# A two-layer decoder trunk: eight conditioning items to VectorE, routing by token tile, first expert outside the loop

## The reference, cut to what matters

```python
def modulate(x, shift, scale):
    return x * (1 + scale[:, None, :]) + shift[:, None, :]

c_act = jax.nn.silu(c)
h = x
for layer in range(2):
    mod = c_act @ w_ada[layer] + b_ada[layer]            # 1024 x 6144, one row
    sh_m, sc_m, gt_m, sh_f, sc_f, gt_f = jnp.split(mod, 6, axis=-1)
    u = modulate(rms_norm(h, g_mix[layer]), sh_m, sc_m)
    y = even_mixer(u, ...) if layer == 0 else dsa_mixer(u, ...)
    h = h + gt_m * y
    u = modulate(rms_norm(h, g_ffn[layer]), sh_f, sc_f)
    y = swiglu(u, ...) if layer == 0 else moe_swiglu(u, ...)
    h = h + gt_f * y
return rms_norm(h, g_final)

def moe_swiglu(u, w_router, b_router, w_gate, w_up, w_down):
    logits = tok @ w_router + b_router                   # 8 experts
    top_val, top_idx = lax.top_k(logits, 2)
    gates = jax.nn.softmax(top_val, axis=-1)
    combine = einsum('tk,tke->te', gates, one_hot(top_idx, 8))
    for e in range(8):
        out = out + combine[:, e:e+1] * swiglu(tok, w_gate[e], w_up[e], w_down[e])
```

## Time and profile before

| | us |
|---|---|
| median of 3 runs | 1614.06 |
| lowest, highest | 1613.65, 1614.63 |
| the profiled execution | 1612.1 |
| its span, first to last instruction | 1610.3 |

### The profile page before, as it was taken

How to read it: one execution, slowest core, us unless ns; L and a number is a source line. 1 busy time by engine, 2 the same in 40 slices (tenths; PEclk the granted TensorE clock), 3 DMA queues, 4 the chain that set the end, 5 groups by cost and what they waited for, 6 DMA issues and landing times.

```text
span 1610.3 us, 21805 instructions
## 1 busy us (share of the span) xinstructions
PE 1517.3 (94%) x7379; PEld 1173.7 (73%) x7380; DVE 1254.9 (78%) x1715; ACT 1047.7 (65%) x1381; POOL 71.9 (4%) x99
## 2 busy tenths in 40 slices
PE   4999989999799878999999999999999999999997
PEld 2645458888585457887887888888888888888885
DVE  6896335544583238989989989989989989989987
ACT  3105444443457527788788788788788788788785
POOL 5251000000000000000000000000000000000000
PEclk9999999999899979999999999999999999999999
DMA  9734975544467657999999999999999999999970
GB/s 305 262 105 177 345 266 204 209 147 171 154 210 248 223 203 263 367 372 351 363 373 349 369 367 349 366 372 360 355 371 366 350 369 364 349 381 365 351 300 28
DMA packets 205176, 474.92 MB, mean 295 GB/s; under 512 B 5252, under 2 KB 11702, under 8 KB 204998
## 3 DMA queue, kind: packets, MB, share of 16 engines
q1 hardware_dynamic: 202656, 466.80, 79.5%
q0 software_dynamic: 1824, 6.33, 1.2%
q10 hardware_dynamic: 646, 1.16, 0.3%
HBM read 472.17 MB, written 2.10 MB: 295 GB/s over the span
## 4 chain that ended last, share of the span: by engine, by line
PE 81%; ACT 5%; DVE 4%; issue 2%; ACTq 0%; DVEq 0%
PE ps L821 23%; PE ps L823 23%; PE ps L822 22%; PE ps L827 3%; DVE w_lo L1972 2%; PE ps L1340 2%; PE ps L1094 2%; ACT work L1868 1%; PE ps L846 1%; ACT uT L1624 1%; ACT w_hi L1611 1%; ACT uT L1633 1%; PE ps L1462 0%; PE ps L866 0%; PE ps L1463 0%
## 5 line engine op out<-in xcount | busy, mean ns | idle before, releaser
L1972 DVE TENSOR_TENSOR w_lo<-ring,w_hi 128x1024 fp32r<-128x1024 f32 (+2 forms) x572 | 665.9, 1200 | 122.9 <-ACT w_hi L1611 104.7
L1611 ACT ACTIVATE w_hi<-ring 128x1024 fp32r<-128x1024 f32 (+2 forms) x572 | 593.0, 1047 | 215.0 <-PE ps L823 211.4
L821 PE MATMUL ps<-w_hi,e_hi 128*128 128x512 f32 x896 | 357.5, 399 | 9.7 <-DVE w_lo L1972 9.7
L823 PE MATMUL ps<-w_hi,e_lo 128*128 128x512 f32 x896 | 350.6, 391 | 0.0
L822 PE MATMUL ps<-w_lo,e_hi 128*128 128x512 f32 x896 | 349.9, 390 | 0.0
L1972 DVE TENSOR_TENSOR w_lo<-ring_more,w_hi 128x1024 fp32r<-128x1024 f32 x192 | 230.5, 1222 | 12.5 <-ACT w_hi L1611 9.7
L1611 ACT ACTIVATE w_hi<-ring_more 128x1024 fp32r<-128x1024 f32 x192 | 202.8, 1061 | 48.6 <-PE ps L823 48.6
L821 PEld LDWEIGHTS ps<-w_hi,e_hi 128*128 128x128 f32 x896 | 168.9, 188 | 46.0 <-DVE w_lo L1972 13.2
L823 PEld LDWEIGHTS ps<-w_hi,e_lo 128*128 128x128 f32 x896 | 168.7, 188 | 36.6
L822 PEld LDWEIGHTS ps<-w_lo,e_hi 128*128 128x128 f32 x896 | 169.2, 189 | 33.2
L821 PE MATMUL ps<-w_hi,eT_hi 128*128 128x512 f32 x448 | 176.7, 394 | 5.6 <-DVE w_lo L1972 5.6
(11 more groups left out here) (286 smaller groups left out, 1566.6 us busy)
## 6 DMA issues: line engine op xcount, KB each, us to landing
ring<-in_moe_w_gate SPq DMA_DIRECT2D x48, 2048.0 KB, 9.7
ring<-in_moe_w_up SPq DMA_DIRECT2D x40, 2048.0 KB, 9.8
ring<-in_moe_w_down SPq DMA_DIRECT2D x32, 2048.0 KB, 8.9
ring<-in_w_ada SPq DMA_DIRECT2D x24, 2048.0 KB, 9.2
ring_more<-in_moe_w_down SPq DMA_DIRECT2D x24, 2048.0 KB, 10.3
ring_more<-in_moe_w_up SPq DMA_DIRECT2D x16, 2048.0 KB, 9.8
ring_more<-in_moe_w_gate SPq DMA_DIRECT2D x8, 2048.0 KB, 7.8
ring<-in_ff_w_gate SPq DMA_DIRECT2D x5, 2048.0 KB, 7.9
```

What stands on the lines that cost most here:

```text
L821: mm(o, xh, wh, start=start, stop=False)
L823: return mm(o, xl, wh, start=False, stop=stop)
L1611: fn(w, src, ACT.Copy).then_inc(hi_ready, 1)
L1972: V.tensor_tensor(w_lo[0:n, c, 0:f], src, w_hi[0:n, c, 0:f].bitcast(F32), ALU.subtract).then_inc(lo_ready, 1)
```

## The change

It has three parts.

1. **Conditioning.** Items 12 to 19 are multiplied by DVE inside the first four feed-forward blocks, two items a block, eight instructions an item (`gemv`); PE adds over partitions and adds the bias at the end of the feed-forward (`gemv_gate` for items 16 and 17 in place of `matvec` 14 and 15, `gemv_columns` for the other six). Items 14 to 19 are loaded between the feed-forward's weights. Items 20 to 23 are left for the attention, in every second head pair. Items 12 to 23 now come in the order shift, scale, gate of the mixer, then shift, scale, gate of the feed-forward. DVE's and SP's loops over blocks are written out. The slots of `e_out`, set free by `matvec` 12 before, are now set free by the first product of `rows_of`.
2. **Routing by token tile.** The logits of tile 0 are computed before tile 1 is transposed, DVE finds its experts at once, and the position products are split. The one-hot matrix of expert 0 comes right after the positions, the combination weights follow it, and the tables of overfull experts (`job_tables`) come after expert 0.
3. **First expert.** ACT and DVE do expert 0 outside their loops. ACT makes the high parts of gate 0 before the softmax of routing, DVE the low parts between the tokens' halves; PE waits for the tokens' halves one by one.

Four items fewer lie in the static stream, so `n_item[0] % 5` is 1 at L539 and `moe_order` becomes slots 1, 2, 3, 4, 0.

```diff
-        parts1 = ada[:, 0:4 * 512].rearrange("p (i n) -> p i n", i=4)
+        parts1 = ada[:, 0:8 * 512].rearrange("p (i n) -> p i n", i=8)
...
-        for (sec, half), back in zip(HALVES[2:4], (3, 1)):
+        for (sec, half), back in zip(HALVES1[2:8], (3, 1) * 3):
             n_item[0] = n_then - back
-            ada_item(1, sec, half)
+            ada_item(1, sec, half, "gemv")
...
-        for sec, half in ((2, 0), (2, 1), (3, 0), (3, 1), (4, 0), (4, 1), (5, 0), (5, 1)):
+        for sec, half in HALVES1[8:]:
             ada_item(1, sec, half)
```

SP, the loads of the feed-forward:

```diff
+            mid_at = {(2 + i // 2, ("down", "up")[i % 2]): e for i, e in enumerate(static_mid)}
+            for b in range(2, FB):
                 for k in FFK:
+                    sp.wait_ge(lo_ready, (b - 2) * CB + (ff_chunks1 + ff_chunk[k] + NCI))
+                    ff_load(k, b, FW if b < FB - 1 else FL)
+                    if (b, k) in mid_at:
+                        load(mid_at[b, k])
...
-            sp.wait_ge(router_done, 1)
+            sp.wait_ge(router_done, 2)
```

PE, the conditioning:

```diff
+            def gemv_columns(i, bank, c):
+                row = ada_items[i][1]
+                mm(ps[bank][:, c:c + 4], bias_rows[0:BROWS, :], ident[0:BROWS, row:row + 4], start=True, stop=False)
+                for q in range(4):
+                    w = mm(ps[bank][:, c + q:c + q + 1], parts1[:, i - 12, q * P:(q + 1) * P], ones[:, 0:1],
+                           start=False, stop=q == 3)
+                return w
+            def gemv_gate(i, bank):
+                pe.wait_ge(gemv_done, i - 11)
+                row = ada_items[i][1]
+                mm(ps[bank][:, :], ones, parts1[:, i - 12, :], start=True, stop=False)
+                for q in range(4):
+                    w = mm(ps[bank][:, q * P:(q + 1) * P], ident[0:BROWS, row + q:row + q + 1].broadcast_to([BROWS, P]),
+                           bias_rows[0:BROWS, :], start=False, stop=q == 3)
+                w.then_inc(mod_summed, 1)
...
-            matvec(12, 2)
...
-            pe.wait_ge(part_ready, 13)
             rows(ff_first["up"][2], (2, 3), FW, range(NCI))
-            matvec(13, 6)
             ff_block(0, True)
...
-            matvec(14, 0)
-            matvec(15, 1)
+            gemv_gate(16, 0)
+            gemv_gate(17, 1)
...
-            pe.wait_ge(part_ready, 16)
+            pe.wait_ge(gemv_done, 8)
             for i in range(4):
-                w = columns_of(12 + i, parts1[:, i, :], 2, 4 * i)
-            w.then_inc(mod_summed, 1)
+                gemv_columns(12 + i, 2, 4 * i)
+            gemv_columns(18, 2, 16)
+            gemv_columns(19, 2, 20).then_inc(mod_summed, 1)
```

PE, the attention, where now only every second pair has a conditioning item:

```diff
-                matvec(16 + pair, 6)
+                if pair % 2 == 0:
+                    matvec(20 + pair // 2, 6)
...
-                ada_step(pair)
+                if pair % 2 == 0:
+                    ada_step(pair // 2)
```

PE, routing:

```diff
+            pe.wait_ge(late_in, 16 * 2)
+            router(0).then_inc(router_done, 1)
             norm(3, 1)
-            pe.wait_ge(late_in, 16 * 2)
-            router(0)
             router(1).then_inc(router_done, 1)
             pe.wait_ge(member_ready, 1)
             mm(ps[5][:, 0:E], tri, member(0), start=True, stop=True)
-            mm(ps[5][:, E:2 * E], tri, member(1), start=True, stop=False)
-            mm(ps[5][:, E:2 * E], ones, member(0), start=False, stop=True)
-            mm(ps[5][:, 2 * E:3 * E], ones, member(0), start=True, stop=False)
-            mm(ps[5][:, 2 * E:3 * E], ones, member(1), start=False, stop=True).then_inc(pos_done, 1)
+            mm(ps[5][:, E:2 * E], ones, member(0), start=True, stop=False)
+            pe.wait_ge(member_ready, 2)
+            mm(ps[5][:, E:2 * E], tri, member(1), start=False, stop=True).then_inc(pos_done, 1)
+            mm(ps[4][:, 2 * E:3 * E], ones, member(0), start=True, stop=False)
+            mm(ps[4][:, 2 * E:3 * E], ones, member(1), start=False, stop=True).then_inc(pos_done, 1)
```

PE, in the gather of expert 0, ahead of `slot_tokens`:

```diff
+                if first:
+                    pe.wait_ge(info_first, 1)
```

PE, in the expert:

```diff
+                        if kind == "gate" and b == 0 and c % 2 == 0:
+                            pe.wait_ge(e_ready, g * 2 + (c // 2 + 1))
-                pe.wait_ge(e_ready, g * 2 + 2)
```

ACT:

```diff
-                if t:
-                    part_out(12, parts1[:, 0, :], 2)
...
-            part_out(13, parts1[:, 1, :], 6)
...
-            part_out(14, parts1[:, 2, :], 0)
-            part_out(15, parts1[:, 3, :], 1)
+            gate_out(0, 0, 0, 10)
+            gate_out(0, 1, 1, 11)
...
+            item_high(moe_c0, 0, moe_fill0[0] + 16, moe_chunk)
             act.wait_ge(gap_ready, 1)
             fn(rt[:, :, 40:41], rt[:, :, 41:42], ACT.Exp).then_inc(gap_exp, 1)
             fn(stat[:, 30:31], eps[:, 0:1], ACT.Silu)
...
-            slots_in(0)
-            slots_high(0)
-            with act.Fori(0, E) as e:
+            for i in range(2):
+                slots_in(0, (i,))
+                slots_high(0, (i,))
+            expert(0, 0, True, True)
+            with act.Fori(1, E) as e:
```

DVE:

```diff
+            def gemv(i, k):
+                (ap, got), _ = ada_items[i]
+                acc = parts1[:, i - 12, :]
+                if k == 0:
+                    dve.wait_ge(fill[got[0]], got[1])
+                    w = V.tensor_scalar(acc, ap[:, 0, :], c_col[:, 0:1], None, ALU.mult)
+                else:
+                    dve.wait_ge(gemv_steps, (i - 12) * (KD - 1) + k)
+                    w = V.scalar_tensor_tensor(acc, ap[:, k, :], c_col[:, k:k + 1], acc, ALU.mult, ALU.add)
+                if k == KD - 1:
+                    w.then_inc(gemv_done, 1)
+                else:
+                    w.then_inc(gemv_steps, 1)
```

DVE, in `ff_block(i)`, with `a = 12 + 2 * i`:

```diff
+                split("gate", 0, (a, 0))
+                split("gate", 1, (a, 1))
                 mids(i * NT, q)
+                split("gate", 2, (a, 2))
+                split("gate", 3, (a, 3))
                 midT_low(i * NT)
+                for c in range(NCI):
+                    split("down", c, (a, 4 + c))
+                for c in range(NCI):
+                    split("up", c, (a + 1, 2 * c), (a + 1, 2 * c + 1))
...
+            gate_low(0, 1)
+            slots_low(0, (0,))
+            gate_low(2)
+            slots_low(0, (1,))
+            gate_low(3)
             step(V.memset(ps[4][:, :], 0.0))
             step(V.memset(ps[5][:, :], 0.0))
...
-            select(0, 0, 0)
-            slots_low(0)
-            with dve.Fori(0, E) as e:
+            expert(0, 1, 0, True, True)
+            job_tables()
+            with dve.Fori(1, E) as e:
```

More of the change, by code:

```diff
@@ L487, in trunk @@
         ff_first = ff_static(("gate", "up"), 0)
-        ada_item(1, *HALVES[0])
+        HALVES1 = [(sec, half) for sec in range(6) for half in range(2)]
+        ada_item(1, *HALVES1[0], "gemv")
         n_item[0] += 1
-        ada_item(1, *HALVES[1])
+        ada_item(1, *HALVES1[1], "gemv")
         static_before = list(stream)
@@ L1861, in _, with slots_in @@
             UF = FB * NT
-            def slots_in(g):
-                for i in range(2):
+            def slots_in(g, halves_=(0, 1)):
+                for i in halves_:
                     act.wait_ge(gather_done, g * 2 + (i + 1))
@@ L2342, in _ @@
                     mask_max(n + 3, selneg)
-                if pair == 6:
-                    columns(1, 1, 16, 7)
+                if pair == 3:
+                    dve.wait_ge(mod_summed, 14)
+                    V.scalar_tensor_tensor(mod_a[:, 1, :], ps[7][:, 0:KD], 1.0, g_col[:, 3, :], ALU.add,
+                                           ALU.mult).then_inc(mod_ready, 1)
             for t in range(NT):
@@ L2360, in _ @@
             for t in range(NT):
-                step(V.max_index(top_i[:, t, :], top[:, t, :], lg[:, t, :]))
-            step.wait()
-            step(V.tensor_copy(rt[:, :, 24:26], top_i[:, :, 0:2]))
-            V.tensor_tensor(rt[:, :, 41:42], top[:, :, 1:2], top[:, :, 0:1], ALU.subtract).then_inc(gap_ready, 1)
-            step.wait()
-            for t in range(NT):
+                dve.wait_ge(router_done, t + 1)
+                chained(V.tensor_tensor(lg[:, t, :], ps[4 + 2 * t][:, 0:E], b_r[:, :], ALU.add))
@@ new lines, in _ @@
+                V.tensor_tensor(rt[:, t, 16:24], rt[:, t, 0:8], rt[:, t, 8:16], ALU.add).then_inc(member_ready, 1)
+            V.tensor_tensor(rt[:, :, 41:42], top[:, :, 1:2], top[:, :, 0:1], ALU.subtract).then_inc(gap_ready, 1)
+            dve.wait_ge(member_ready, 2)
+            dve.wait_ge(pos_done, 1)
+            for t in range(NT):
+                step(V.scalar_tensor_tensor(possel[:, t, 0:E], ps[5][:, t * E:(t + 1) * E], 1.0, rt[:, t, 16:24], ALU.add, ALU.mult))
+            step.wait()
@@ new lines, in _ @@
+            chained(V.tensor_scalar(possel[:, :, 0:E], possel[:, :, 0:E], -1.0, None, ALU.add))
+            dve.wait_ge(pos_done, 2)
+            for t in range(NT):
+                w = V.tensor_scalar(sel[:, t, :], iota(P), possel[:, t, 0:1], None, ALU.is_equal)
+                if t == 0:
+                    step(w)
```

(17 more changed lines are left out.)

138 lines of the change are left out of this document (61 added, 77 removed).

## The result

The changed kernel takes 1598.39 us (median of four runs, 1597.3 to 1600.59) against 1614.35 (four runs) for the kernel before on the same chip: ratio 0.9898, 95% interval 0.9886 to 0.9911. I had forecast 1590.5 and a range of 1584.0 to 1597.5. The sign is right, the gain is not: 16 us where 23.6 were promised, and the median lies 0.9 us above the range.

The account below looks back on a forecast made before the run. PE was taken to bound feed-forward and experts, ACT and PE taking turns in the attention; 8.8 + 1.0 + 8.0 + 7.0 - 1.2 = 23.6 us off 1614.06 gave 1590.5, range 1584 to 1597.5.

Parts of the forecast that it names:

- Entry: Start of the feed-forward: without items 12 and 13 on PE, 2.0 and 5.1 us gained, plus 1.7 of clock, 8.8 in sum.
- The clock term: First feed-forward block: PE's clock rises from a mean 0.95 to full because PE is never idle, 1.7 us gained.
- Inside the blocks: Feed-forward blocks: DVE's sixteen added instructions at 0.77 us stay hidden, DVE 29.2 of 33.5 us busy, cost 0.
- Rival (a): Feed-forward: DVE becomes the bound, dependent instructions taking 1.49 us each, 29 us more in four blocks, 1619.5; chance 0.04.
- Rival (d): Feed-forward: ring items land late for DVE and stall PE, 2 us in each of three blocks, 1596.5; chance 0.08.
- End of the feed-forward: Behind the two gemv_gate: full-width products recover part of 1.6 us lost to PE's low clock, 1.0 us gained.
- gemv_columns hidden: After the feed-forward: 30 products, 6.8 us, up to 9.5 at the lower clock, lie in PE's 7.45 us wait, cost 0.
- Attention: Pairs 1, 3 and 5 lose ACT copies and waits, 5.1 us; last pair 1.8, pair 6 1.1; 8.0 gained in sum.
- Rival (c): ACT's waits in the attention stay in another place, or gate 0 lands late: 4 us less gain, 1594.5; chance 0.2.
- Routing: Output projection's end to first expert: gather earlier, then gate 0's landing, high parts and table loads; PE starts 7.0 us earlier.
- Rival (b): Gate 0 doesn't hold back the first expert, or lands before ACT needs it: 4.5 us more gain, 1586; chance 0.15.
- Seam: Between experts 0 and 1: job_tables moves there, eight dependent DVE steps of 0.2 us, 1.2 of 1.6 us lost.

Follow-up runs that it names:

- best: Changed kernel with gate_early's slots, job tables made in DVE's idle routing time, and two unread wide products per attention pair without an item: 1589.99 us, ratio 0.9845.
- gemv_twice: Changed kernel with each DVE multiply-add of the eight feed-forward conditioning items done a second time into unread columns: 1606.15 us.
- warm_attn: Changed kernel with two unread 512-column PE products added to each attention head pair without a conditioning item: 1596.07 us, ratio 0.9883.
- gate_first: Changed kernel with the load of gate 0 issued ahead of down 0, same slot and still when the projection ends: 1595.17 us, ratio 0.9865.
- gate_early: Changed kernel with output projection items in ring slots 4 and 3, so slot 0 is free early for gate 0: 1594.05 us, ratio 0.986.
- tables_idle: Changed kernel with job_tables moved from between experts 0 and 1 to DVE's wait for ACT's exponentials in routing: 1598.7 us, ratio 0.9889.
- warm_wait: Changed kernel with unread 512-column PE products between and behind the gemv_columns items after the feed-forward: 1603.72 us, ratio 0.9927.

## Why the prediction was right and wrong

**Entry, 8.8 promised, 7.8 measured.** Both profiles have one spell of 3.4 us, so the 7.8 is what the products of items 12 and 13 and the wait behind them gave, where 2.0 + 5.1 = 7.1 were worked out. The clock term failed: I gave the whole 1.7 us because PE would never idle there. It still waits for the norm of tile 1, until 220.10, and the spell lies there. In best there is none, and the entry takes 40.01, a gain of 9.2. The clock term was right as a bound and wrong as a forecast.

**Inside the blocks, 0, right.** Of sixteen instructions fourteen last 0.747 us and two 0.48; one behind another whose output it needs starts 0.78 after it, against 0.77 estimated, and all are hidden. Rival (a) fell by that 0.78, where it needed 1.49. Its mild form, the flush of the Trainium skill (VectorE: DVE Perf Modes, The DRAIN you can't avoid), fell too: it was an estimated 1.22 us from start to start, and the trace shows 0.78 with a dependence and 0.66 without. That section itself adds that an operation that is not held starts earlier, and the trace agrees. gemv_twice, which makes DVE the bound, shows that the cover is real and that 6.3 us of a block are left of it. Rival (d), items late in the ring, cost nothing: DVE waited for them 1.6 us in all and PE did not.

**End of the feed-forward, 1.0 promised, 2.2 in the table, 0.5 of it the change.** Three of the four profiles of before have 3.4 us at low clock there (70.3 to 70.4 us), the fourth has not (68.72). After the change three profiles with that spell read 69.8 to 69.9, the others 68.2. Like with like is 0.5 us. The rest goes with the spell, which three of four profiles of before have and three of twelve with the change; whether the change makes it rarer is open. "Nearer the gain because full-width products now stand where narrow ones did" was no reason.

**gemv_columns hidden, wrong in its consequence.** The 30 products did lie in PE's wait, from 407.52 to 417.2, 9.7 us where 6.8 to 9.5 were said. What I left out is that the stretch behind could itself come out at the low clock, 2.0 us worse. That this follows from the columns alone was my next theory, and the runs took it away; the long form is usual with the change and in none of the four profiles without it; by which part of the change is open.

**Attention, 8.0 promised, 6.2 measured.** Rival (c)'s first half, the waits staying in another place, did not happen. The mechanism is right: pairs without an item take 4.25 to 4.53 us where 5.94 - 1.7 = 4.24 were expected, and the pairs with an item stay near 6. The size is off in two places. The last pair takes 6.60 us where I had 5.74; 0.66 of that is the clock (warm_attn). The rest is two or three tenths in the later pairs, and ACT's timeline shows where they are:

```profile
509.85 0.37 ACT L1660 ACTIVATE work<-ps 128x256 f32<-128x256 f32 x1
...
512.24 0.49 ACT L1666 ACTIVATE uT<-ps 128x384 f32<-128x384 f32 x1 [0.20 <-PE ps L828]
...
517.89 0.60 ACT L1579 ACTIVATE gate_row<-ps 128x512 f32<-128x512 f32 x1 [0.90 <-PE ps L886]
```

In a pair without an item 0.20 of the 1.16 us of waiting stays. The first such pair has no copy of 256 columns (L1660, 0.26 us in the chain of waits) and so takes 4.25 instead of 4.53. The two pairs of 6.13 are those of items 22 and 23, whose gate ACT waits for and copies.

**Output projection, 0 promised, -2.2 measured.** This is the step that failed outright: TensorE's clock behind the attention, a term that I put at nothing. I read the attention as ACT's, wrote that the conditioning products there only held ACT up, and costed them on ACT's side alone. The 43.86 us of PE's busy time in the earlier trace rows became 32.65, and the clock went with it. The fall begins in the last pair and lasts 6.8 us; it costs 2.9 us in pair and projection together, and with that alone undone (warm_attn, 1596.07) the time lies inside my range.

**Routing, 7.0 promised, 6.3 measured.** Right step by step up to the landing: gate 0 landed after 16.2 us (14.7 taken), four high parts in 3.90, two table loads of 1.28 with the next instruction 0.01 to 0.02 us behind, PE 26.8 us behind the projection (26.1 forecast). The 1.5 us by which the landing was later than its row of before is the 0.7 missing, and more. Rival (b), that gate 0 is no hindrance, fell in gate_first and gate_early: it cost 5.2 us, where I had 4.5. What cost them was its place behind down 0 in the queue, since gate_first changes that alone. By the Trainium skill (ScalarE: Activation LUTs, What ACT_TABLE_LOAD costs), with its drain at each table switch, the term was an estimated 4.2; the trace has two switches and no drain, and 6.3 is nearer the row's 7.0.

**Seam, -1.2 promised, -1.15 measured**, and put down to its cause by tables_idle.

**The sum.** 9.4 us were missing in the profiled execution: 1.9 start (chance), 1.0 entry, 2.0 ahead of the attention, 1.8 attention, 2.2 projection, 0.7 routing, 0.9 the other experts and the end (0.7 of it in the last 56 us, where a low-clock spell shows too), less 1.2 won at the feed-forward's end. The profiled execution of the changed kernel lies 0.5 us below its median, that of before 2.2 below its 1614.35, which gives the medians' 16. The range was too narrow for one reason: I treated TensorE's clock as something that a change can only give back. Behind the attention it took 2.9 us, and the cause is shown; ahead of the attention it took 2.0, and the cause is open. That the feed-forward's end gave more than promised is the luck of one spell. Rival (c) went this way by half the size, for another cause.

## What to carry to other kernels

Work taken from an engine that has room may still have been paying for its clock: when products leave a stretch that another engine bounds, read PEclk of the stretch behind it, and count a loss there as a term of the sum. Weights that the next stage needs first should be issued ahead of others that are let go at the same moment: second of two, gate 0 landed after 16.2 us, first of two after 7.9, and the earlier slot of gate_early gave no more than that order. And before a two-microsecond term is explained, take a second and a third profile: one that fits is not a cause.

## What had not been expected of the hardware

One stretch that the change hardly touches has two lengths, 77.9 and 80.0 us, with nothing between in all its profiles, and which one it is goes with the moment at which the clock fell (0.4 to 1.1 us ahead of the residual, or 1.4 to 1.7). The clock fell in warm_wait with PE busy in every microsecond (16.10 of 16.10):

```profile
407.90:424.00 16.10, 16.10 (x75) 14.65 (x76) 11.22 (x19) 3.29 (x7) 0.00 (x0) 0.60 0.60 215
```

And two unread products for each of four pairs, some 6 us of PE's time, made the attention and the projection 2.9 us shorter. The medians of the two whole kernels agree in sign, but their intervals overlap.
